# An input projection in seven block products, four token passes and mixers that follow them

## The reference

```python
h = rmsnorm(x, norm_g)                              # (tokens, 1024)
z = einsum('btd,de->bte', h, w_in)                  # one projection, 3460 columns
q_a, k_att, v_a, f_a, g_a, sh_b, g_b, u_c, g_c, u_d, g_d = split_cols(z)
logf = log_sigmoid(f_a + fox_bf)
o_a = attend(qh, kh, vh, logf)                      # A: forgetting attention, 4 heads of 64, paged cache for samples
xm = sh + rw_mu * (prev - sh)                       # B: token shift over 896 columns, two loras, decays, key norms,
o_b, wkv1, shift1 = rwkv7_mix(sh_b, ...)            #    then a recurrence on a 64x64 state per head
win = cs[:, w:] - cs[:, :-w]; o_c = pool_mixer(...) # C: windows of 2, 4, 8, 16 tokens, from a running sum
glu = u1 * sigmoid(u2)                              # D: 31-tap depthwise convolution, LayerNorm, swish,
o_d = silu(norm(conv(glu))) @ pw_out                #    a 256x256 product
mixed = concat([o_a * silu(g_a), o_b * silu(g_b), o_c * silu(g_c), o_d * silu(g_d)])
x = x + mixed @ w_out                               # then a final rmsnorm
```

## Time and profile before

| | |
|---|---|
| median of 3 runs | 1674.02 us (1671.11 to 1678.54) |
| span of the profiled execution | 1668.8 us |
| PE busy | 1612.8 us, 97% |
| DVE busy | 806.7 us, 48% |
| ACT busy | 487.3 us, 29% |
| POOL busy | 127.0 us, 8% |
| mean of the DMA engines' traffic | 181 GB/s |

### The profile page before, as it was taken

How to read it: one execution, slowest core, us unless ns; L and a number is a source line. 1 busy time by engine, 2 the same in 40 slices (tenths; PEclk the granted TensorE clock), 3 DMA queues, 4 the chain that set the end, 5 groups by cost and what they waited for, 6 DMA issues and landing times.

```text
span 1668.8 us, 32594 instructions
## 1 busy us (share of the span) xinstructions
PE 1612.8 (97%) x13510; PEld 967.5 (58%) x13510; DVE 806.7 (48%) x1782; ACT 487.3 (29%) x946; POOL 127.0 (8%) x166
## 2 busy tenths in 40 slices
PE   6999999999999999999999999999899999999998
PEld 3555555555555555558745666668788764444443
DVE  5560199974212234533066676644454549343333
ACT  5301100001106352410245565553233353010001
POOL 1100000002100000000000000000000003222220
PEclk9999999999999999999999999999999999999999
DMA  7232332137541315581266546567676559999983
GB/s 264 73 132 98 119 106 72 66 120 192 171 129 64 142 38 217 198 292 63 88 181 191 149 137 185 179 201 224 190 217 183 182 192 361 353 332 352 356 321 130
DMA packets 150797, 302.87 MB, mean 181 GB/s; under 512 B 16725, under 2 KB 121381, under 8 KB 132278
## 3 DMA queue, kind: packets, MB, share of 16 engines
q1 hardware_dynamic: 128714, 155.65, 29.8%
q0 software_dynamic: 17280, 117.18, 19.7%
q10 hardware_dynamic: 4656, 27.96, 4.1%
HBM read 237.88 MB, written 65.10 MB: 182 GB/s over the span
## 4 chain that ended last, share of the span: by engine, by line
PE 78%; DVE 12%; ACT 4%; DMA 4%; issue 2%; SPq 1%; ACTq 0%; DVEq 0%
PE psum L875 29%; PE psum L1134 24%; DVE big L1901 9%; PE psum L846 5%; PE psum L956 4%; PE psum L1094 4%; PE psum L1012 4%; PE psum L1080 3%; PE psum L901 2%; PE psum L1439 2%; ACT big L1557 2%; DMA pars<-zT 1%; DMA big<-in_xT 1%; PE psum L1342 1%; PE psum L943 1%
## 5 line engine op out<-in xcount | busy, mean ns | idle before, releaser
L875 PE MATMUL psum<-big,wbuf 128*128 128x416 f32 x1920 | 677.7, 514 | 12.2 <-DVE big L1807 10.8
L875 PEld LDWEIGHTS psum<-big,wbuf 128*128 128x128 f32 x1920 | 365.3, 191 | 318.6 <-issue 313.4
L1134 PE MATMUL psum<-big 64*64 64x64 f32 (+4 forms) x5440 | 256.0, 269 | 14.1 <-issue 7.4
L1134 PEld LDWEIGHTS psum<-big 64*64 64x64 f32 (+2 forms) x5440 | 176.9, 132 | 99.3 <-issue 73.3
L1530 ACT ACTIVATE zst<-psum 128x416 f32<-128x416 f32 x123 | 63.0, 517 | 522.4 <-PE psum L875 522.3
L1901 DVE SCALAR_TENSOR_TENSOR big<-big,pars 128x2048 f32<-128x2048 f32 x120 | 148.2, 1298 | 1.1
L746 POOL DMA_INDIRECT big<-in_cache_v,pidx x64 | 69.7, 1090 | 682.7 <-PE psum L1094 468.5
L846 PE MATMUL psum<-ident,big 128*128 128x128 f32 (+1 forms) x556 | 78.7, 280 | 7.5 <-ACT big L1711 3.3
L1080 PE MATMUL psum<-wbuf,big 128*64 128x128 f32 x544 | 77.0, 281 | 0.6 <-ACT big L1680 0.3
L1080 PE MATMUL psum<-big 128*64 128x128 f32 x544 | 77.0, 282 | 0.0
L846 PEld LDWEIGHTS psum<-ident,big 128*128 128x128 f32 (+1 forms) x556 | 61.2, 145 | 26.5 <-issue 13.1
(11 more groups left out here) (311 smaller groups left out, 1690.0 us busy)
## 6 DMA issues: line engine op xcount, KB each, us to landing
big<-in_k_pages SPq DMA_DIRECT2D x432, 128.0 KB, 2.3
zT<-zst ACTq DMA_DIRECT2D x25, 1040.0 KB, 6.1
wbuf<-in_w_slots SPq DMA_DIRECT2D x24, 512.0 KB, 4.1
big<-zT POOLq DMA_DIRECT2D x11, 1024.0 KB, 5.6
zst<-in_k_pages SPq DMA_DIRECT2D x80, 128.0 KB, 2.7
rwS<-big POOLq DMA_DIRECT2D x8, 1024.0 KB, 4.2
big<-rwS SPq DMA_DIRECT2D x8, 1024.0 KB, 5.7
out_y_prompt<-big SPq DMA_DIRECT2D x16, 512.0 KB
```

Of the source, the lines that this page charges most:

```text
L875: last = nc.tensor.matmul(psum[:, m % CHUNKS, 0:CW], w[:, k, :], x, start=(k == 0), stop=(k == KT - 1))
L1134: return nc.tensor.matmul(out, l, r, start=start, stop=stop, skip_group_check=True)
```

## The change

The projection is done in another algorithm and in another order of loops. Tokens are taken in four passes of 512 (the first 544, with the samples). Slots are taken in 12 pairs, a pair and a pass being a unit `U`. In a unit the weights are a 2 by 2 block matrix (two slots, two halves of the features) and so are the tokens (two halves of the features, two halves of the pass), and the four block products of z are made from seven products of sums of blocks instead of eight: `product(p, i, j, ...)`, j from 0 to 6, each 4 k-steps of 256 columns (272 in the first pass). Products 3, 4 and 5 add onto the PSUM banks of products 0, 1 and 2. The sums of weight blocks are made by POOL in every unit (`weight_sums`, four operations of 128x512), the sums of token blocks by DVE once in a pass (`token_sums`, four of 1024). ACT copies the seven results to `parts_` (`copies`), which lies in `zst` and is two units deep; DVE adds them up to z in `evac`, 5 additions of 256 (7 where samples are in the unit). Eight of the pairs go on without a way through HBM: the mixers C, D and the elementwise part of B now run on DVE within a pass, on 512 tokens, with the last tokens of the pass before carried in the row. Only keys, queries and the gates of A and B go to `zT`. Buffer names: `w_pair` the two pairs of slots, `w_sums` POOL's results, `hb` the tokens (two passes deep), `t_sums` the token sums. The scan rows, token shift and key norms of a pass stand at fixed units; `TAPS` says how many of D's 31 taps stand behind each unit. `decode_queries` on DVE and its products on PE come behind the third attention item; D's variance and its pointwise product of the last pass come behind the last product on PE.

The core of the diff:

```diff
+PASSES, PT_W, UNITS = 4, 512, 12
...
+PAIR_COLS = (2180, 2692, 2948, 1028, 1284, 1540, 3204, 2436, 256, 0, 772, 1924)
...
+            def weights(U):
+                if U >= 2:
+                    sp.wait_ge(prod, 7 * (U - 1))
+                sp.dma_start(w_pair[U % 2][:, :, :, :], I['w_pairs'][U % UNITS]).then_inc(w_in[U % 2], 16)
...
+                    if U + 2 < UNITS * PASSES:
+                        weights(U + 2)
+                    else:
+                        sp.wait_ge(prod, 7 * (U + 1))
...
+            def kq_load(c0, c1, s):
+                sp.dma_start(kq[:, :, :, :].rearrange("p m t c -> p (m t) c")[:, :, c0:c1], zT[KA:QA + 2].rearrange("r p c -> p r c")[:, :, c0:c1]).then_inc(s, 16)
+            sp.wait_ge(z_stored[0], z_stores(3, 8))
+            sp.wait_ge(z_stored[1], z_stores(3, 9))
+            sp.wait_ge(rw_stored, 64 * PASSES)
+            sp.wait_ge(pool_stored, stores(3))
+            sp.wait_ge(v_stored, stores(3))
+            kq_load(0, 512, kq_in)
+            sp.wait_ge(nc_ready, 1)
+            sp.dma_start(ncD, nc_[:, 0:SEQ]).then_inc(nc_kept, 16)
+            sp.wait_ge(nc_kept, 16)
+            sp.dma_start(ck_first, ncD[:, 0:512].unsqueeze(0).to_broadcast([P, 4, 512])).then_inc(ck_in[0], 16)
             sp.dma_start(dmask, I['diag_mask']).then_inc(rows_in, 16)
...
+            sp.wait_ge(lo_stored, 16)
+            sp.wait_ge(prod, 7 * UNITS * PASSES)
             sp.dma_start(ck_rest, ncD[:, 512:SEQ].unsqueeze(0).to_broadcast([P, 4, SEQ - 512])).then_inc(ck_in[1], 16)
+            kq_load(1024, SEQ, kq_rest)
...
+            store_conv(3)
+            for to, src in ((O['poolE'].rearrange("t p c -> p t c")[:, :, 0:POOL_BUF], halo_c), (O['convE'].rearrange("t p c -> p t c")[:, :, 0:CONV_BUF], halo_d),
+                                           (O['shiftP'], halo_e)):
+                sp.dma_start(to, src).then_inc(out_stored, 16)
+            sp.wait_ge(conv_stored, stores(3))
+            sp.wait_ge(z_stored[1], z_stores(3, 11))
+            sp.dma_start(scores_[:, 1:], lfD.rearrange("b h r c -> (b h) (r c)").unsqueeze(1).to_broadcast([32, 4, N_PAGES * PAGE])).then_inc(lf_stored, 16)
...
+            def weight_sums(U):
+                u = U % 2
+                w, s = w_pair[u], w_sums[u]
+                pool.wait_ge(w_in[u], 16 * (U // 2 + 1))
+                if U >= 2:
+                    pool.wait_ge(prod, 7 * (U - 1))
+                g.tensor_tensor(s[0], w[:, 1, 0:4, :], w[:, 1, 4:8, :], ALU.add).then_inc(sums_ready, 1)
+                g.tensor_tensor(s[1], w[:, 0, 0:4, :], w[:, 1, 0:4, :], ALU.subtract).then_inc(sums_ready, 1)
+                pool.wait_ge(sums_ready, 4 * U + 2)
+                g.tensor_tensor(w[:, 1, 0:4, :], s[0], w[:, 0, 0:4, :], ALU.subtract).then_inc(sums_ready, 1)
+                pool.wait_ge(sums_ready, 4 * U + 3)
+                g.tensor_tensor(s[2], w[:, 0, 4:8, :], w[:, 1, 0:4, :], ALU.subtract).then_inc(sums_ready, 1)
+            for U in range(UNITS * PASSES):
+                weight_sums(U)
+                if U == 0:
...
-                for k in range(KT):
...
-                    last = nc.tensor.matmul(psum[:, m % CHUNKS, 0:CW], w[:, k, :], x, start=(k == 0), stop=(k == KT - 1))
...
+            def product(p, i, j, bank, left, right, first=True):
+                U = UNITS * p + i
+                if j < 3:
+                    if U >= 1:
+                        pe.wait_ge(z_cp, 7 * U - 3 + j)
+                elif j < 6:
+                    pe.wait_ge(z_cp, 7 * U + j - 2)
+                elif U >= 1:
+                    pe.wait_ge(z_cp, 7 * U)
+                for k in range(4):
+                    last = nc.tensor.matmul(psum[:, bank, 0:wide(p) // 2], left(k), right(k), start=first and k == 0, stop=k == 3, skip_group_check=True)
+                last.then_inc(prod, 1)
...
+                n = wide(p) // 2
+                pe.wait_ge(w_in[U % 2], 16 * (U // 2 + 1))
+                if i == 0:
+                    pe.wait_ge(hn_ready, hn_through(p, 1))
+                product(p, i, 0, 0, lambda k: w[:, 0, k, :], lambda k: h[:, k, h0])
+                pe.wait_ge(sums_ready, 4 * U + 1)
+                pe.wait_ge(t_ready, 4 * p + 1)
+                product(p, i, 1, 1, lambda k: s[0][:, k, :], lambda k: t_sums[0][:, k, 0:n])
+                pe.wait_ge(sums_ready, 4 * U + 2)
+                pe.wait_ge(t_ready, 4 * p + 2)
+                product(p, i, 2, 2, lambda k: s[1][:, k, :], lambda k: t_sums[2][:, k, 0:n])
+                pe.wait_ge(sums_ready, 4 * U + 3)
+                pe.wait_ge(t_ready, 4 * p + 3)
+                product(p, i, 3, 0, lambda k: w[:, 1, k, :], lambda k: t_sums[1][:, k, 0:n], False)
+                pe.wait_ge(sums_ready, 4 * U + 4)
+                product(p, i, 4, 1, lambda k: s[2][:, k, :], lambda k: h[:, 4 + k, h1], False)
+                pe.wait_ge(t_ready, 4 * p + 4)
+                product(p, i, 5, 2, lambda k: w[:, 1, 4 + k, :], lambda k: t_sums[3][:, k, 0:n], False)
+                product(p, i, 6, 3, lambda k: w[:, 0, 4 + k, :], lambda k: h[:, 4 + k, h0])
+            def wa_columns(p, h):
+                pe.wait_ge(wa_in, 16 * (p + 1))
+                x = x_raw if p == 0 else hb[p % 2]
+                b = bank_of(('WA', p, h))
...
+            def copies(p, i, first, last):
+                U = UNITS * p + i
+                n = wide(p) // 2
+                for j in range(first, last):
+                    if j == 0 and U >= 2:
+                        act.wait_ge(z_add, adds_through((U - 2) // UNITS, (U - 2) % UNITS))
+                    act.wait_ge(prod, 7 * U + j + 1)
+                    nc.scalar.activation(parts_[:, U % 2, j, 0:n], psum[:, (0, 1, 2, 0, 1, 2, 3)[j], 0:n], ACT.Copy, scale=0.125 if i == U_QA else 1.0).then_inc(z_cp, 1)
...
+                if i == 4 and p + 1 < PASSES:
+                    for h in HALVES:
+                        inverse_root(p + 1, h)
...
+            def token_sums(p):
+                n = wide(p) // 2
+                h, h0, h1 = hb[p % 2], half(p, 0), half(p, 1)
+                if p > 0:
+                    dve.wait_ge(prod, 7 * UNITS * p)
...
+                dve.wait_ge(z_cp, 7 * U + 3)
+                v.tensor_tensor(s[:, M5], s[:, M5], s[:, M7], ALU.add).then_inc(z_add, 1)
...
+                dve.wait_ge(z_cp, 7 * U + 5)
+                total(0, 1, s[:, U2_], s[:, X_])
+                dve.wait_ge(z_cp, 7 * U + 6)
+                total(1, 0, s[:, U2_], s[:, Y_])
+                dve.wait_ge(z_add, done)
+                total(1, 1, s[:, U2_], s[:, M5])
+                dve.wait_ge(z_cp, 7 * U + 7)
+                total(0, 0, s[:, M1], s[:, M2])
...
+        TAPS = ((0, 0, 5, 4, 4, 4, 6, 8), (0, 0, 5, 4, 4, 4, 6, 8), (0, 0, 5, 4, 4, 4, 6, 8), (0, 0, 2, 2, 5, 5, 8, 9))
...
+                    token_sums(p)
+                    conv_gated(p - 1)
...
+                    if i == 6:
+                        key_norms(p)
+                    evac(p, i)
...
+                    if i in (3, 4, 5):
+                        mix_pair(p, i)
+                    if 2 <= i <= 7:
+                        taps_at(p, i)
```

1732 lines of the change are left out of this document (976 added, 756 removed).

## The result

| | before | after |
|---|---|---|
| median | 1673.35 us (4 runs) | 1751.19 us (1749.74 to 1754.73, 4 runs) |
| ratio | | 1.0458, 95% interval 1.0436 to 1.0480 |
| span of the profiled execution | 1668.8 | 1748.0 |

The account below looks back on a forecast made before the run. The projection was taken to be bound by PE's matmuls. The span of 1668.8 - 78 + 50 + 32 + 6 gave 1678.8 us, and the median, 5.2 above its span, 1684 us; the range was 1634 to 1735.

Parts of the forecast that it names:

- Products, -78: Projection on PE: 1920 records taking 670.1 us become 2688 narrower ones taking 591.5, saving 78 us.
- The exclusion: Projection: POOL's sums, 1.2 us each, and DVE's two-input SBUF operations cannot overlap, so their times add up.
- What of it PE feels, +50: Projection: PE stalls on late DVE after 9 us of slack per pass, plus 3 for late sums; 50 us.
- Nothing for the order and the clock: Projection: DVE alone keeps up, 96.5 us against PE's 109 in passes 1 or 2; no term for order or clock.
- The handover, +32: Projection to attention: 12.5 MB of loads, a gate row and key page issues delay item 5; 32 us lost.
- ACT, +6: Projection: function changes at 1.28 us per table load, for norms, loras and gates, cost 6 us.
- No exclusion: Rival 1: POOL's sums hidden beside DVE in the projection; 1634 us, or 1644 with POOL at 0.87; chance 27%.
- Rival 2: Projection: a POOL sum takes 1.6 us or waits for groups of taps, and PE waits; 1742 us; chance 16%.
- The case's own range: Whole kernel: 1665 us (POOL at 0.95, handover 21) to 1705 us (POOL at 1.35); forecast case, chance 45%.

Follow-up runs that it names:

- the second profile of the same kernel: The changed kernel, unaltered, run and profiled again on the same chip as three later variants; 1746.8 us, ratio 1.0463 to the kernel before.
- the fastest version: The kernel with the two orders, 1664.7 us, ratio 0.9981; its follow-up with first key pages issued behind item 3's store measured 1669.5 us, 0.9977.
- 336 sums: Changed kernel with three of each unit's four weight sums made twice by POOL; 1867.9 us, ratio 1.1201.
- the kernel with the two orders: DVE sums kept in HBM, D's mean later, reworked handover; plus C's products read at unit 8's end, D's rows stored earlier: 1664.7 us, 0.9981.

## Why the prediction was wrong, and where it was right

- **Products, -78.** Measured -84, of which 4 only moved behind the last product. The pace carried over from the 260-wide and 416-wide records: a unit of 56 records takes 12.08 us from start to start, 0.216 a record against 0.217 forecast. Right.

```profile
285.01 12.25 PE L1023 MATMUL psum<-big 128*128 128x256 f32 x56
297.09 7.07 PE L1057 MATMUL psum<-big 128*128 128x256 f32 x32
```

- **The exclusion.** The mechanism was read rightly from one POOL instruction of 7.17 us beside the earlier trace rows, and the price of a sum too: 1.26 us against 1.2 forecast from two fills and one operation that reads the earlier trace rows. The Trainium skill (GPSIMD Engine Reference, Elementwise — side-by-side cycle accounting) gives an estimated 1.1; the measurement decides. The one instruction showed only POOL waiting. That DVE waits too, 150 of the 223 us, stood in no row of before and is first shown by the run with POOL writing only.
- **What of it PE feels, +50.** The step that failed, in its path more than in its size. I let PE's slack be the depth of the parts, one unit or 9 us, and expected waits before products 1 to 3, released by ACT's copies. Those waited 2.5 us in all. PE's queue is in order and has some 30 small products in each pass that need DVE's or ACT's latest result, with four banks between them all; there PE waited. The term was 69 us, 58 of idle time and 11 of clock.
- **Nothing for the order and the clock.** The second failure, and the larger in the sum: 47 us, where 6 stood for ACT. With POOL reading nothing PE still waits 32 us more than before and loses 15 to the clock. I had checked that DVE's work of a pass fits (96.5 of 109 us) and took that for "no wait". The sum over units says nothing about the place of one result. Moving the mean, and then the reading of four banks, gave 32 us with the exclusion in force, so a part of what the exclusion costs comes through these places too. I did not cost the clock at all; 13 waits or groups of them were each followed by 1.4 to 3.1 us lost at lower clock.
- **The handover, +32.** Measured +47, and +38 in the second profile of the same kernel; the upper bound was 33 + 12. Of the 47, 7 are lower clock, which the term didn't have. (The sum for item 5 has a slip: 46 + 9.0 + 2.2 is 57 us and not 59.) The terms (gate row behind the logs, key pages' issues of 9.0) were the right ones at first. SP's queue in the changed kernel, and the two finishes:

```profile
921.97 0.57 SPq L774 DMA_DIRECT2D big<-lfD  x1
...
923.23 0.42 SPq L748 DMA_DIRECT2D pars<-zT  x1
...
936.28 9.41 SPq L785 DMA_DIRECT2D big<-in_k_pages  x16
```

```profile
935.38 0.29 DVE L2498 TENSOR_TENSOR pars<-psum,pars 128x128 f32<-128x128 f32 x1 [9.28 <-DMA pars<-zT]
...
954.14 0.29 DVE L2498 TENSOR_TENSOR pars<-psum,pars 128x128 f32<-128x128 f32 x1 [9.89 <-DMA pars<-zT]
```

  Item 5 is done 66 us behind the last product, against 22 before and 47 to 59 forecast. "Late because of traffic" was half of it. What I left out: three small outputs hold SP's queue for 10.5 us, and the store of D's rows stands behind the large loads.
- **ACT, +6.** About right: with POOL writing only, PE waited 5.4 us for ACT at the loras and 2.5 for copies. A table load still took 1.28 us and the next function began 1.29 us behind its start (157.71 and 159.00 us there). The earlier trace rows has only the load; the function behind it is this one, also 1.29 us later:

```profile
827.43 0.26 ACT L1557 ACTIVATE big<-big 128x68 f32<-128x68 f32 x1
```

  The 2.66 us of the Trainium skill (ScalarE: Activation LUTs, What ACT_TABLE_LOAD costs) shows at neither place.
- **The rivals.** No exclusion would have given 1634 by my sum; without it the kernel is at 1.0043, some 1681 on the scale of the first median, 47 us off, by the waits and the clock of the fourth point above and by the handover. Rival 2's time, 1742, was near, but for neither of its reasons: a sum takes 1.26 us by itself, its mean of 1.64 being the wait for DVE, and PE never waited for one. That the time came near it is luck.
- **The case's own range** has a slip as well: with POOL at 0.95 us and the handover at 21 the prediction's own terms give about 1643 us and not 1665. The measured time lies on the other side.
- **The sum as measured:** -84 + 69 + 47 + 47 = +79, 1668.8 to 1748.

Open: what the handover of the fastest version still costs, 844 to 853 us behind its last product against 813 before. It is not the place of the key pages. DVE waits there 13 to 14 us for the 3 MB of prefix while the DMA engines are busy 0.99 of the time, so for these bytes at this place it is traffic. Before, the 4 MB of logs came in during the projection; here they overwrite D's last rows and can't. Ahead of the last product the fastest version also still has 32 us more idle time of PE than before (48.5 against 16.7).

## What to carry to other kernels

Before an elementwise step goes to an idle engine, ask whether it and the busy engine would read SBUF at the same time: here giving four additions a unit back to the busier engine made the kernel 43 us faster. When work is cut into passes, check where each small result is wanted, in its consumer's order, and which bank or store stands before it; a budget per pass doesn't show that, and two moved calls gave back more than a third of what the products saved. Where a transfer is waited for, look at the share of the DMA engines in that stretch: at 0.99 another order of the queue only changed which load was late, and only the hole at 0.61 was a small store queued behind large loads.

## What the runs showed of the hardware

- Two-input operations of POOL and DVE out of SBUF cost the sum of their times: 223 of 242 us, and 415 of 423 with 336 sums. With an input in PSUM DVE's are untouched (686 to 688 ns).
- Not only two-input ones were hit. DVE's copies of 60 columns within SBUF (L2200) took 670 ns in the changed kernel and 195 with POOL writing only, and a 512-column operation with one tensor and two columns of parameters (L2270) 1017 against 644. With POOL silent (sums on DVE) the latter took 544, so for it POOL's writes cost something too. Another of that kind, a tap's first (L2216), stayed at 546 to 547 in all three; why is open. In the changed kernel:

```profile
L2270 DVE TENSOR_SCALAR big<-big,pars,one_m_ka 128x512 f32<-128x512 f32 x6 | 6.1, 1017 | 0.0
...
L2200 DVE COPY big<-big 128x60 f32<-128x60 f32 x4 | 2.7, 670 | 0.2
```

- A wait of PE is dearer than it looks: 107 us of idle time came with 26 us lost at lower clock, and 106 with 34 in the second profile, a quarter to a third on top.
- With its transfers queued behind 9 MB, SP was held 30 us by 16 issues of key pages that take 8 to 9 elsewhere (the kernel with the two orders):

```profile
839.87 29.95 SPq L797 DMA_DIRECT2D big<-in_k_pages  x16
```
